# Heads stage of a streaming encoder trunk: in the slots with a chunk, the other group's inversion step is issued ahead of the chunk's first product

## The reference

```python
def wkv_step(S, inp):
    r_t, w_t, k_t, v_t, a_t, b_t = inp
    sa = jnp.einsum('bhvk,bhk->bhv', S, a_t)
    S = S * w_t[:, :, None, :] + sa[..., None] * b_t[:, :, None, :] + v_t[..., None] * k_t[:, :, None, :]
    y = jnp.einsum('bhvk,bhk->bhv', S, r_t)
    return S, y
...
    S_final, ys = lax.scan(wkv_step, wkv_prev.astype(jnp.float32),
                           (tm(rh), tm(wh), tm(kh), tm(vh), tm(-kk), tm(bh)))
```

## Time and profile before

| | us |
|---|---|
| median of 3 runs | 2707.68 (2706.12 to 2709.07) |
| the profiled execution, its own time | 2709.8 |
| its span | 2708.0 |
| PE busy | 2553.1 (94% of the span) |
| DVE busy | 1667.5 (62%) |
| POOL busy | 1584.2 (58%) |
| ACT busy | 958.4 (35%) |

### The profile page before, as it was taken

How to read it: one execution, slowest core, us unless ns; L and a number is a source line. 1 busy time by engine, 2 the same in 40 slices (tenths; PEclk the granted TensorE clock), 3 DMA queues, 4 the chain that set the end, 5 groups by cost and what they waited for, 6 DMA issues and landing times. The chain is left out here.

```text
span 2708.0 us, 65806 instructions
## 1 busy us (share of the span) xinstructions
PE 2553.1 (94%) x27280; PEld 2459.3 (91%) x27280; DVE 1667.5 (62%) x2420; ACT 958.4 (35%) x2014; POOL 1584.2 (58%) x1303
## 2 busy tenths in 40 slices
PE   8999999978888999999999999998888899999997
PEld 8999999967777999999999999988777789999996
DVE  6867238655554789931598971576555548899124
ACT  3444013444532245410245530244455314454002
POOL 6556666733324677666767766666234256776664
PEclk9999999989998999999999999999999989999998
DMA  4222332100000232233322322321000013222322
GB/s 151 95 102 85 89 101 74 63 3 5 4 20 27 87 108 94 93 87 91 93 98 94 103 81 87 101 72 39 4 4 5 27 48 101 94 95 84 88 89 77
DMA packets 81897, 193.65 MB, mean 72 GB/s; under 512 B 13680, under 2 KB 14064, under 8 KB 81648
## 3 DMA queue, kind: packets, MB, share of 16 engines
q1 hardware_dynamic: 78192, 187.07, 21.5%
q10 hardware_dynamic: 3456, 3.02, 0.4%
HBM read 186.95 MB, written 3.12 MB: 70 GB/s over the span
## 5 line engine op out<-in xcount | busy, mean ns | idle before, releaser
L850 PE MATMUL ps<-xa,w_hi 128*128 128x272 f32 x2208 | 583.4, 289 | 4.0 <-DVE w_lo L1745 2.4
L850 PE MATMUL ps<-xa,w_lo 128*128 128x272 f32 x1932 | 560.6, 290 | 0.0
L850 PE MATMUL ps<-xb,w_hi 128*128 128x272 f32 x1656 | 478.9, 289 | 0.0
L642 POOL TENSOR_SCALAR w_hi<-w_raw 128x1024 fp32r<-128x1024 f32 (+2 forms) x225 | 241.3, 1072 | 402.7 <-PE ps L736 394.4
L850 PEld LDWEIGHTS ps<-xa,w_hi 128*128 128x128 f32 x2208 | 399.1, 189 | 6.2 <-DVE w_lo L1745 3.0
L646 POOL TENSOR_TENSOR w_lo<-w_raw,w_hi 128x640 fp32r<-128x640 f32 (+2 forms) x225 | 367.1, 1632 | 0.0
L850 PEld LDWEIGHTS ps<-xa,w_lo 128*128 128x128 f32 x1932 | 364.2, 189 | 0.0
L850 PEld LDWEIGHTS ps<-xb,w_hi 128*128 128x128 f32 x1656 | 312.7, 189 | 0.0
L736 PE MATMUL ps<-hh,w_hi 128*128 128x272 f32 x1472 | 304.9, 288 | 5.6 <-DVE hl L1773 5.4
L736 PE MATMUL ps<-hh,w_lo 128*128 128x272 f32 x1472 | 302.7, 288 | 0.0
L736 PE MATMUL ps<-hl,w_hi 128*128 128x272 f32 x1472 | 302.3, 287 | 0.0
(11 more groups left out here) (351 smaller groups left out, 5693.6 us busy)
## 6 DMA issues: line engine op xcount, KB each, us to landing
w_raw<-in_wz SPq DMA_DIRECT2D x44, 512.0 KB, 3.2
w_odd<-in_w1i SPq DMA_DIRECT2D x72, 256.0 KB, 2.9
w_odd<-in_w2i SPq DMA_DIRECT2D x72, 256.0 KB, 2.9
w_raw<-in_w1i SPq DMA_DIRECT2D x68, 256.0 KB, 2.9
w_raw<-in_w2i SPq DMA_DIRECT2D x64, 256.0 KB, 2.8
w_raw<-in_w1o SPq DMA_DIRECT2D x32, 448.0 KB, 3.3
w_raw<-in_w2o SPq DMA_DIRECT2D x32, 448.0 KB, 3.3
w_raw<-in_w2i SPq DMA_DIRECT2D x20, 512.0 KB, 3.3
```

The costliest lines, as they stand in the source:

```text
L642: pool.tensor_scalar(w_hi[k][:, 0:nk, :], w_raw[k][:, 0:nk, :], 1.0, 0.0, ALU.mult, ALU.add).then_inc(w_hi_done, 1)
L850: mm = pe.matmul(ps[:, bank(site, b, j), 0:HT], w, x, start=(j in FRESH and k + i == 0), stop=(k == 3 and i == 2), skip_group_check=True)
```

## The change

In the slots with a chunk, `chunk_in` is moved behind the step, on PE and on DVE. On PE the order becomes step, chunk_in, state_y, chunk_out, chunk_y; on DVE it becomes the step's output, um, S. ACT, POOL and SP are as they were.

```diff
@@ PE, half_a @@
-                    if right and k >= 5:
-                        chunk_in(k - 1, l, p - 1)
                     if left and k == 0:
...
                     elif left:
                         step(k - 3, 0, n)
                     if right and k >= 5:
+                        chunk_in(k - 1, l, p - 1)
                         state_y(k - 1, l, p - 1)
                         chunk_out(k - 1, l, p - 1)
                         chunk_y(k - 1, l, p - 1)
@@ PE, half_b @@
                     if k < 5:
                         step(7 + k, 0, n)
-                    elif k < 9:
-                        chunk_in(k - 5, l, p)
...
                     else:
                         step(k - 3, 1, n)
                     if 5 <= k < 9:
+                        chunk_in(k - 5, l, p)
@@ DVE, half_a @@
-                    if right and k >= 5:
-                        chunk_in(k - 1, n - 1)
...
                     if left and k >= 3:
                         step(k - 3, 0, n)
                     if right and k >= 5:
+                        chunk_in(k - 1, n - 1)
                         chunk_out(k - 1, l, p - 1)
@@ DVE, half_b @@
-                    elif k < 9:
-                        chunk_in(k - 5, n)
...
                     if k >= 3:
                         step(k - 3, 1, n)
                     if 5 <= k < 9:
+                        chunk_in(k - 5, n)
                         chunk_out(k - 5, l, p)
```

## The result

The changed kernel takes 2745.49 us (2745.22 to 2746.54, 4 runs) against 2706.9 us: ratio 1.0146, interval 1.013 to 1.0162. It is 38.6 us slower, where 30.4 were forecast. In a second comparison of the same two kernels, among the experiments, it is 30.4 us slower (2738.24 against 2707.8, ratio 1.0107, 1.0081 to 1.0133). The profiled execution of after has a span of 2743.5 us, 35.5 more than before's.

What follows compares the result with a forecast made beforehand. The heads stages were taken as bound by a chain of short PE groups and DVE or ACT answers. Half_b 12.7, half_a 16.9 and 0.8 sum to 30.4 us: 2707.7 + 30.4 = 2738, own range 2731 to 2745, widened 2723 to 2751.

Steps and rivals of the forecast that it cites:

- nothing absorbs the shift: Heads stages: each delayed step feeds the next, so no absorption was counted; rival of no change, chance 0.02.
- X slots of five blocks: Half_b's slots sharing a 20-record step with a chunk: 2.13 us forecast against 1.72, so +0.41 each.
- X slots of four: Half_a's slots sharing a 16-record step with a chunk: 1.95 us forecast against 1.62, so +0.33 each.
- "0.52": Slot's last term on PE: the next group starts 0.52 us after the second product's first matmul.
- the forecast 0.97 in half_b: Half_b's delay after two slots of 2.13 us: its third X slot at 634.78 instead of 633.80.
- the G16 slot: Slot 6, just ahead of the X slots, step output on ACT, so um doesn't queue: 1.73 us forecast in half_a.
- the forecast was 1.49: Half_a, after the slot with 32 records and the sample chunk: next step at 660.03 instead of 658.54, +1.49 us.
- forecast 1.69: End of half_a: DVE's tA, which PE's head sum needs, at 660.28 instead of 658.59, +1.69 us.
- ACT's copy of the y tile: Half_b: copy moves +1.1 us and delays the G32 output PE needs; +1.1 for 8 of 12 half_b, +0.97 for 4.
- The 47.5 us: PE's idle before the first chunk product, waiting 119 times for DVE's S; forecast to fall to nearly nothing.
- The step output and um: DVE in X slots: um starts 0.42 us after a five-block step output, 0.36 after four blocks; um itself lasts 0.28.
- a rival with 0.14: Clock rival: thin PE stretches bring one more clock fall per pair, up to 20 us, middle 10: 2748; chance 0.14.

Runs made afterwards that it cites:

- the pair of one-sided orders: The change on PE only, DVE as before: 2696.66 us; the change on DVE only, PE as before: 2791.94 us (kernel before: ratios 0.9952 and 1.0302).
- the fillers: Matmuls nobody reads, added to the changed kernel where PE waits, in two versions: 2727.01 and 2726.59 us, ratios 1.0065 and 1.0062 against the kernel before.
- the filled pair: Unread matmuls where PE waits, added to the kernel before (2703.28 us) and, with more in the waits for um, to the changed kernel (2727.01 us).
- the half_b runs: The change on PE and DVE in half_b only, half_a as in the kernel before: 2718.43 us, ratio 1.0033.
- PE's order alone: The change on PE only, DVE's order as in the kernel before: 2696.66 us (0.9952), again 2696.46 us (0.9966).
- either half: The change on PE and DVE in one function only, against the kernel before: half_a 2719.93 us (1.0042), half_b 2718.43 us (1.0033).

## Why the prediction was right

**The mechanism was the one predicted**, and the pair of one-sided orders shows it: the covered wait for S comes back as a wait for um behind the step's output. Undoing DVE's half of the change takes 21 of the 24.6 us away; doing DVE's half alone costs about 45. The forecast that nothing absorbs the shift held too: what a half loses, the next mark still shows.

**The sum was 30.4 and the slots cost 24.6.** Point by point: X slots of five blocks were put at 2.13 us and take 2.05 from b to b, X slots of four at 1.95 and take 1.97 and 1.89. The mis-sized term is the last, "0.52" from the second product to the next step. It is 0.41 and 0.29 in half_b (637.33 to 637.74, 639.52 to 639.81) and 0.40 and 0.29 in half_a (659.00 to 659.40, 660.63 to 660.92), because the next step's matmuls already start between those of chunk_y. A part of this is given back, since a step whose first matmuls stand among others takes up to 0.16 longer. What is left makes 0.90 of the forecast 0.97 in half_b. In half_a it takes the G16 slot from the forecast 1.73 to 1.52 (659.40 to 660.92), and the next step comes 1.34 later (667.50 - 656.29 = 11.21 from b, for 658.54 - 648.67 = 9.87 before), where the forecast was 1.49. At half_a's end tA took 0.78 us for 1.08, so of its own delay of 1.57 (forecast 1.69) 1.3 was lost.

Two more terms were off. ACT's copy of the y tile did move by 1.1 us (from 633.88 at the earlier trace rows to 640.25, with the pair 5.24 later anyway), but PE didn't wait for ACT: half_b lost 0.90 with and without the scaling of y. That term, 8 x 0.13 = 1.0 us, was empty. And the first half_b of a layer was forecast like the others and lost 0.69: there the G16 slot, which no longer waits for S, brings X1's output 0.4 us ahead instead of 0.2.

**A reading was off.** The 47.5 us of "PE stood idle" are PE's 21.8 and PEld's 25.6 together. The forecast of over 40 us of wait for um was PE's alone and came true with 42.6 (50.0 with ums); the sum doesn't use the 47.5, so it isn't touched.

**The step output and um** were sized well: 0.41 for 0.42 from b to um for an even chunk. For an odd chunk it is 0.52 (638.65 to 639.17), b's whole 0.49 and more. The Trainium skill ("VectorE: DVE Perf Modes", "Two Vector instructions with no wait between them") states that an instruction which starts in another quadrant than the last one is held until the earlier ones have finished, and the trace agrees: 0.11 us in each of 22 slots, 2.4 us, which the prediction had put at 1.5 and left out of its sum.

**The clock was left to a rival with 0.14 and a middle of +10 us.** It did come with the forecast case instead of in place of it: 14 us in the first comparison (38.6 - 24.6), 6 in the second. The prediction named "the clock falls in most pairs" as a sign that it would be wrong, and that sign came: in the profile of after the clock falls in seven of the twelve pairs, in before's in two (counted as above, without the falls at a layer's start and in its last half_a). That the second comparison gives the forecast 30.4 us to the tenth is luck: an error of -5.8 in the slots and one of +6 for the clock cancel. In the first comparison they don't, and its 2745.49 us lie half a us above the forecast's own 2731 to 2745. So the mechanism in the slots was right and its size a quarter too large, and the clock's share was missing from the sum. That the changed kernel has falls where the fillers take them out is shown; that the wider waits for um bring them is argued from the windows and from the filled pair, and the half_b runs speak against it as the whole reason, since they have these waits in half_b and no more half clock than before.

**Open:** PE's order alone is 10 us faster in two comparisons, with slots 3.8 us longer. Where the time comes from is shown: 22 executions have 71 and 76 us at half clock on the mean, 81 of before have 112, and 39 us x 0.35 = 14 us, less 3.8, is the gain. In the profiles the difference is mostly the long fall in the last half_a. Why the clock falls less often there, behind an order that changes only the slots ahead, stays open; so does why the full change has more falls than either half.

## What to carry to other kernels

A wait that you move off one engine's queue is gone only if nothing else in its chain now queues: follow the covered operation to its reader, and look at what stands ahead of it on the other engine. When an order is changed on two engines, time each half alone; here PE's half cost 3.8 us in the slots and DVE's half more than both together. Take fixed costs from marks in stretches where the granted clock is 1.00, and price the clock separately, from the clock and time of every execution and not of the profiled one alone, because it shifts the total by more than a small change is worth.

## What the runs showed of the hardware

- Matmuls that nobody reads, put where PE waited (behind X3 and in the last half_a), made the kernel before 0.5% faster (2695.95 us for 2707.8): in the stretch shown the granted clock stayed at 2.4 GHz.
- Falls of the clock aren't fixed by the code: two stretches of equal instructions, 8.37 and 8.19 us busy of 13.4, had 20.5 us at 1.2 GHz behind one and none behind the other, and the 81 executions of before spent from 86 to 147 us at half clock.
- In this program a us at 1.2 GHz costs 0.35 us of time (slope over 200 executions, standard error 0.01), less than the half that it would cost if PE were never waiting.
- On DVE an instruction behind a step output of 0.49 us started 0.41 us after it when both began at the same partition, and 0.52 us after it when it began at partition 64 (637.01 and 639.17 us in after).
- POOL and DVE slow each other down. tA on DVE mostly took 1.06 to 1.08 us in before while POOL multiplied y, and those two POOL instructions took 3.12 us; in after, with tA at their end, 0.78 and 2.63 us. POOL in before, then in after:

```profile
657.73 3.12 POOL L672 TENSOR_TENSOR y<-y,rsz 128x544 f32<-128x544 f32 x2
```
```profile
665.35 2.63 POOL L672 TENSOR_TENSOR y<-y,rsz 128x544 f32<-128x544 f32 x2
```
